# A fused decoder step on one NeuronCore: value pages of the second phase issued by GpSimd, and value quads moved ahead of the levels

## The chip, the cores and the metric

One NeuronCore of a Trainium2 chip runs the whole program. The metric is the device time of one launch in microseconds (us), the median of several runs. The profile is one more execution, taken by the hardware profiler. Engines are TensorE (PE, and PEld for its weight loads), VectorE (DVE), ScalarE (ACT), GpSimd (POOL) and SyncE (SP); SP only issues transfers here. SPq and POOLq are the sequencers of SP and POOL.

## What is computed

One layer of a hybrid decoder for a prompt of 2048 + 16 tokens and for 8 sampled sequences of one token each, all in float32. The part that matters here is the sampled sequences' attention over 8192 cached positions, which lie in pages of 128 positions x 512 floats (256 KB), found through a page table:

```python
xn = rms_norm(h, norm_w)
rq, rf, ri, rg, aq, ak, av, ag = split(xn @ w_in)        # 8 projections of 512 columns
o_rec = hgrn2_scan(rq, k_in(rf), ri, log_f(rf), S0)      # gated linear recurrence, 4 heads
k_all = concat(cache_k[page_table], ak)                  # 64 pages of each sampled sequence
v_all = concat(cache_v[page_table], av)
p = softmax(q @ k_all.T / 8)                             # two maps of each head
o_att = (p[0] - lam * p[1]) @ v_all
y = concat(rms_norm(o_rec) * silu(rg), rms_norm(o_att) * silu(ag))
out = h + y @ w_out
```

## The kernel before, in words

The prompt is cut into 16 tiles of 128 tokens and goes through two phases. The first phase (tiles 0 to 15) does the prompt's causal attention; the second (again tiles 0 to 15, then a tail of 24 rows) does its recurrence, in eight "levels" of a chunk, and the output projection. The eight sampled sequences run as side work beside both: 32 steps of 16 pages, four steps a sequence, where step `it` is tile `it` of the first phase and tile `it - 16` of the second. In each step VectorE multiplies 16 key pages with the query and sums (eight "key slots" of two pages, `key_slot`, L1361 and L1366, one buffer `Kt` of two slots), and TensorE multiplies 16 value pages of the sequence before it with its softmax weights, in four "value quads" of four pages (`value_quad`, L512). Tiles whose number is a multiple of 4 are the "opening" ones, where the side work changes to another sequence.

The value buffer `Vt` holds exactly one quad: four pages, in two halves. The next quad's pages may be asked for only when the quad before has been multiplied (semaphore `v_used`), and the quad waits at its head until both halves have landed. TensorE issues in order, so a late page stops all that stands behind the quad.

Who issues the pages. In the first phase SP issues key pages (`slots` with `ORDER_K`, L2100), and POOL issues value pages (`value_pages`, L1958: four page numbers are read into registers, a wait on `v_used`, four transfers). In the second phase SP issues both, in an order written out by hand (`ORDER_B`), one queue: `K0 V0 V1 K1 K2 K3 K4 K5 V2 V3 K6 V4 V5 K7 V6 V7`, where each name is a pair of pages. Ahead of K6 stands `turned_x` (L2152), the load of the input tile after next, 512 KB, which waits until all four projections of the present tile are done. POOL's own work in the second phase is little: it stores the finished output rows (L2062, L2069, L2070, after a wait on VectorE's final normalization L1751), waits for that store, loads the residual rows of a later tile (`load_x`, L357 and L358) and loads the attention output (L2067, after TensorE's transposes L820).

TensorE's order in a tile of the second phase (`b_tile`), non-opening: projections 1 and 0 (L747, 32 matmuls each), a wait, projection 3, quad 0, eight transposes (L762), projection 2, then level 0 (L863, and transposes L820) and levels 1 to 7 (four small matmuls each, L868). Behind levels 1, 2, 3 and 5 stands a quarter of the output projection of the tile before (L831), and behind levels 1, 4 and 7 stand quads 2, 4 and 6. Then come transposes (L881), the outputs (L888, L889) and the state update (L894). In an opening tile quad 0 stands inside `opening_front`, behind projection 3. VectorE makes each level's operands (L1799, L1800), takes each level's result (L2217), and works off key slots in between; in a non-opening tile key slot 6 stands ahead of level 2's operands.

In the first phase the order on TensorE around a tile's heads is written in `filler`, `scores` (L451, L456), `turn` (L465) and `values` (L480); the next tile's projections (`project_a`, L411) and the value quads are its fillers. In tiles 8 to 15 a head's row is cut into two pieces (c = 0 and 1); VectorE's `join` makes the piece's weights (L1412, L1413 for c = 0, L1416 for c = 1) and `norm_a` (L1422 to L1432) normalizes the tile before, and releases the first `values` of the tile by the semaphore `normed`. POOL's order there, for each tile t: pages of quad 0, store of xT and K, then in tile 14 the load of next-phase weights W[1] and W[0] (`next_weights`, L1966, 2 MB each, which wait for the last use of the weights they replace), the attention store (L2000, after `normed`), pages of quad 2 and quad 4, the store of V, and again in tile 14 W[2], pages of quad 6, W[3].

## Time and profile before

| | |
|---|---|
| time before, median of 3 runs | 2221.23 us (2218.32 to 2232.84) |
| the profiled execution | 2214.55 us, its span 2212.7 us |
| TensorE, VectorE, ScalarE, GpSimd busy | 90%, 73%, 23%, 10% of the span |
| mean granted TensorE clock | 0.950 |
| moved by DMA | 356.52 MB, mean 161 GB/s |
| first phase, second phase and tail | 0 to about 1101 us, about 1101 to 2212.7 us |

The median is 6.7 us above the profiled execution. Times in the rows are from the start of the span. "Idle before" is the time for which the engine stood still just ahead of an instruction, and the arrow names what ended it.

### The profile page before, as it was taken

Reading aid. Unit: us, or ns where it says so; the run is one execution under the profiler, and the core shown is the slowest. Engines: PE = TensorE matmul, PEld = TensorE weight load, DVE = VectorE, ACT = ScalarE, POOL = GpSimd, SP = SyncE. Lnnn points to the kernel's source line nnn. Section 1 sums busy time; section 2 is a strip of 40 time slices with the busy share of each in tenths; the row PEclk is TensorE's granted clock in tenths of the full one; section 3 lists DMA queues with packets and bytes.
Section 4 is the critical chain, followed back from the end, with each engine's and each line's share of the span. In section 5 each row is a group of like instructions: output and inputs, shape, how many; then the busy total and the mean of one; then the engine's idle time right before and its main releaser. Section 6 shows DMA issues by size and latency. Waiting matters only on the chain.

```text
span 2212.7 us, 31467 instructions
## 1 busy us (share of the span) xinstructions
PE 1981.8 (90%) x9530; PEld 1203.9 (54%) x9530; DVE 1623.0 (73%) x3477; ACT 518.9 (23%) x1280; POOL 229.0 (10%) x443
## 2 busy tenths in 40 slices
PE   6899999987989899877779999999989999999987
PEld 3444445543544454434557666666657766667443
DVE  2588778776777787758667886888778886888653
ACT  1233333332433343333301111111111111111100
POOL 0000122111111111011120000000000000000020
PEclk9999999999999999988889999999999999999988
DMA  6254466634534334454355553555545553655663
GB/s 223 92 167 148 149 217 201 198 116 141 168 125 148 124 118 136 143 181 167 124 174 166 177 174 109 191 177 177 175 138 178 175 186 105 195 174 173 185 213 119
DMA packets 165757, 356.52 MB, mean 161 GB/s; under 512 B 21040, under 2 KB 25920, under 8 KB 165600
## 3 DMA queue, kind: packets, MB, share of 16 engines
q1 hardware_dynamic: 131536, 240.41, 34.1%
q0 software_dynamic: 34064, 114.19, 15.6%
q8 instruction: 77, 1.26, 0.2%
q14 instruction: 80, 0.66, 0.1%
HBM read 322.52 MB, written 32.00 MB: 160 GB/s over the span
## 4 chain that ended last, share of the span: by engine, by line
PE 35%; DVE 8%; DMA 5%; SPq 2%; issue 2%; ACT 0%; DVEq 0%; ACTq 0%
PE PS L747 18%; PE PS L831 5%; DMA Vt<-in_cache_v_dram 4%; PE PD L512 3%; DMA Kt<-in_cache_k_dram 2%; DVE Kt L1361 2%; DVE sc L1366 2%; SPq L2100 1%; PE PS L744 1%; PE PS L868 1%; PE PO L888 1%; PE PS L948 1%; PE PO L889 1%; PE PS L894 1%; PE PS L906 1%
## 5 line engine op out<-in xcount | busy, mean ns | idle before, releaser
L411 PE MATMUL PT<-W,xT 128*128 128x512 f32 x960 | 432.9, 599 | 1.2 <-ACT xT L1008 1.1
L1361 DVE TENSOR_TENSOR Kt<-Kt,qb 128x1024 f32<-128x1024 f32 x256 | 312.2, 1219 | 42.9 <-DMA Kt<-in_cache_k_dram 42.4
L1366 DVE TENSOR_REDUCE sc<-Kt 128x16 f32<-128x1024 f32 x256 | 312.2, 1220 | 8.0
L747 PE MATMUL PS<-W,normw 128*128 128x256 f32 x1024 | 308.6, 383 | 0.0
L411 PEld LDWEIGHTS PT<-W,xT 128*128 128x128 f32 x960 | 177.3, 192 | 192.7 <-issue 190.6
L831 PE MATMUL PS<-region 128*128 128x512 f32 x512 | 232.1, 596 | 3.6 <-ACT region L1236 3.5
L747 PEld LDWEIGHTS PS<-W,normw 128*128 128x128 f32 x1024 | 197.5, 193 | 27.7
L1045 ACT ACTIVATE Pr<-PS,negm 128x512 f32<-128x512 f32 (+7 forms) x192 | 165.6, 866 | 163.3 <-DVE negm L1380 146.3
L512 PE MATMUL PD<-Vt,pst 128*8 128x512 f32 x912 | 123.8, 615 | 55.4 <-DMA Vt<-in_cache_v_dram 55.3
L456 PE MATMUL PS<-region,Q 64*128 64x512 f32 (+3 forms) x640 | 161.7, 620 | 0.0
L747 PE MATMUL PS<-W,xbuf 128*128 128x256 f32 x512 | 158.3, 392 | 0.8 <-DVE oX L1662 0.8
L1382 DVE TENSOR_REDUCE negm<-PS 128x1 f32<-128x640 f32 (+3 forms) x64 | 65.4, 1021 | 123.5 <-PE PS L456 123.5
L480 PE MATMUL PO<-region,PTs 128*128 128x128 f32 x1088 | 145.8, 284 | 7.3 <-issue 6.4
L747 PE MATMUL PS<-W,xT 128*128 128x256 f32 x512 | 152.3, 379 | 0.0
L480 PEld LDWEIGHTS PO<-region,PTs 128*128 128x128 f32 x1088 | 135.5, 197 | 26.5 <-issue 14.2
L831 PEld LDWEIGHTS PS<-region 128*128 128x128 f32 x512 | 92.3, 190 | 97.8 <-issue 91.8
L1958 POOL DMA_DIRECT2D Vt<-in_cache_v_dram x192 | 103.9, 541 | 363.5 <-PE PD L512 292.7
L1062 ACT ACTIVATE PTs<-PT 128x512 f32<-128x512 f32 (+3 forms) x160 | 85.2, 533 | 237.0 <-PE PT L465 233.3
L465 PEld LDWEIGHTS PT<-ident,Pr 128*128 128x128 f32 x544 | 65.3, 150 | 138.7 <-issue 127.3
L465 PE MATMUL PT<-ident,Pr 128*128 128x128 f32 x544 | 98.7, 301 | 40.4 <-DVE Pr L1413 37.5
L1380 DVE TENSOR_REDUCE negm<-PS 128x1 f32<-128x1024 f32 (+7 forms) x128 | 103.6, 851 | 39.3 <-PE PS L456 38.5
L747 PEld LDWEIGHTS PS<-W,xbuf 128*128 128x128 f32 x512 | 97.8, 196 | 21.1 <-issue 6.8
(377 smaller groups left out, 2348.8 us busy)
## 6 DMA issues: line engine op xcount, KB each, us to landing
Kt<-in_cache_k_dram SPq DMA_DIRECT2D x512, 256.0 KB, 3.6
Vt<-in_cache_v_dram SPq DMA_DIRECT2D x264, 256.0 KB, 3.6
Vt<-in_cache_v_dram POOLq DMA_DIRECT2D x192, 256.0 KB, 4.3
W<-in_w_in_dram SPq DMA_DIRECT2D x4, 2048.0 KB, 18.9
xT_scratch<-xT POOLq DMA_DIRECT2D x16, 512.0 KB, 6.2
W<-in_w_in_dram POOLq DMA_DIRECT2D x4, 2048.0 KB, 9.0
region<-in_x_prompt_dram POOLq DMA_DIRECT2D x16, 448.0 KB, 4.5
out_dram<-region POOLq DMA_DIRECT2D x16, 448.0 KB, 4.0
```

Source lines behind the costliest of these rows:

```text
L411: mm = pe.matmul(Pj, xT[:, c, :], W[:, b, c, :], start=(c == 0), stop=(c == DC - 1))
L456: mm = pe.matmul(PS[:, 2 * s + a, 0:n], Q[rows, h, :], KT[rows, h, first + o:first + o + n], start=not ends, stop=True, skip_group_check=ends)
L465: mm = pe.transpose(Pw[:, u:u + P], Pr[:, PLACE[t, h, c][0], o + u:o + u + P], ident[:, :])
L480: mm = pe.matmul(PO[:, h * P:(h + 1) * P], PTs[:, n % 2, u * P:(u + 1) * P], V[:, k + u, h * P:(h + 1) * P], start=(k + u == 0), stop=(k + ...
L512: mm = pe.matmul(PD[32 * j:32 * j + HC, :], pst[:, (2 * s + j) * HC:(2 * s + j + 1) * HC], ring[:, j // 2, j % 2, :], start=False, stop=Fa ...
L747: mm = pe.matmul(PS[:, BANK[b], a], rowsx, W[:, b, c, a], start=(c == 0 and a.start == 0), stop=(c == DC - 1), skip_group_check=True)
L831: mm = pe.matmul(PS[0:rows, b, :], yTs[:, c, 0:rows], Wo[:, c, b * G:(b + 1) * G], start=(c == 0), stop=(c == DC - 1))
L1045: act.activation(Pr[:, PLACE[t, h, c][s], 0:w], pair(s, w), ACT.Exp, bias=negm[:, h % 2, c, s:s + 1], accum_out=total).then_inc(p_done, 1)
L1361: link(ve.tensor_tensor(kp, kp, qb[:, :].unsqueeze(1).to_broadcast([P, 2, G]), ALU.mult))
L1366: ve.tensor_reduce(sc[:, g % 2, bass.ds(r16, 2), :].rearrange("p a c -> p (a c)"), kp.rearrange("p a (c d) -> p (a c) d", d=64), X, ALU.ad ...
L1380: ve.tensor_reduce(m, pair(s, w), X, ALU.max, negate=True).then_inc(m_done, 1)
L1958: pool.dma_start(Vt[:, u // 2, u % 2, :], vc[bass.ds(page, 1), :, :].rearrange("a t n -> t (a n)")).then_inc(va_load[u // 2], 16)
```

## The change

POOL issues the value pages of the second phase too: `value_pages` is no longer cut off at t = 16, and its calls stand in POOL's second-phase program between the stores and loads that are there already. SP is left with the key pages, and `turned_x` stays ahead of K6. The unused orders and the semaphores `v_load` go. The quads of a second-phase tile move: quad 0 of a non-opening tile stands behind projection 1, quad 2 behind projection 3 (in an opening tile behind projection 2), quad 4 behind level 1 (opening: 2), quad 6 behind level 5. In the first phase's tile 14 POOL takes the pages of quad 2 ahead of W[0] and the pages of quad 6 ahead of W[2], and W[3] goes to tile 15, behind the pages of quad 0. On VectorE, `norm_a` of the tiles 8 to 15 stands behind the join of the second piece, where it stood ahead of it.

```diff
@@ value_quad (TensorE)
                     for half in range(2):
-                        if g < 4:
-                            pe.wait_ge(va_load[half], (it * 4 + (s // 2 + 1 - 16)) * 32)
-                        else:
-                            pe.wait_ge(v_load[half], (it * 4 + (s // 2 + 1 - 64)) * 32)
+                        pe.wait_ge(va_load[half], (it * 4 + (s // 2 + 1 - 16)) * 32)
@@ b_tile (TensorE)
                 else:
-                    project(n, (1, 0))
+                    project(n, (1,))
+                    value_quad(it, 0, g)
+                    project(n, (0,))
                     pe.wait_ge(s_upd, after(t + 0, ONE_ON))
                     project(n, (3,))
-                    value_quad(it, 0, g)
+                    value_quad(it, 2, g)
                 qk_transposes(n)
                 project(n, (2,))
+                if t % 4 == 0:
+                    value_quad(it, 2, g)
...
-                    if l in (1, 4, 7):
-                        value_quad(it, {1: 2, 4: 4, 7: 6}[l], g)
+                    if l == (2 if t % 4 == 0 else 1):
+                        value_quad(it, 4, g)
+                    elif l == 5:
+                        value_quad(it, 6, g)
@@ first phase (VectorE)
                         join(t, h, 0)
+                        join(t, h, 1)
                         if h == 0:
                             norm_a(t - 1)
-                        join(t, h, 1)
@@ value_pages (GpSimd)
-                if t < 4 or t >= NT:
+                if t < 4:
                     return
@@ first phase (GpSimd)
                 value_pages(t, 0)
+                if t == NT - 1:
+                    next_weights(3)
...
                 if t == NT - 2:
                     next_weights(1)
-                    next_weights(0)
...
                 value_pages(t, 2)
+                if t == NT - 2:
+                    next_weights(0)
                 if t % 4:
                     value_pages(t, 4)
...
-                if t == NT - 2:
-                    next_weights(2)
                 if t % 4 == 0:
                     value_pages(t, 4)
                 value_pages(t, 6)
                 if t == NT - 2:
-                    next_weights(3)
+                    next_weights(2)
...
+            value_pages(NT, 0)
             pool.wait_ge(pv_done, NB + 5)
@@ second phase (GpSimd), behind the masks
+            value_pages(NT, 2)
+            value_pages(NT, 4)
+            value_pages(NT, 6)
+            value_pages(NT + 1, 0)
+            value_pages(NT + 1, 2)
+            value_pages(NT + 1, 4)
             pool.wait_ge(y_tr, 2)
             pool.dma_start(ycat[:, G:D], y_att_dram[1]).then_inc(ya_load, 16)
+            value_pages(NT + 1, 6)
+            value_pages(NT + 2, 0)
...
             for t in range(1, NT - 1):
+                value_pages(NT + t + 1, 2)
+                if (t + 1) % 4:
+                    value_pages(NT + t + 1, 4)
                 pool.wait_ge(y_tr, 2 * t + 2)
                 pool.dma_start(ycat[:, G:D], y_att_dram[t + 1]).then_inc(ya_load, 16)
+                if (t + 1) % 4 == 0:
+                    value_pages(NT + t + 1, 4)
+                value_pages(NT + t + 1, 6)
+                if t + 2 < NT:
+                    value_pages(NT + t + 2, 0)
                 pool.wait_ge(y_out, t + 1)
@@ second phase (SyncE)
-                slots(t + NT, ORDER_B, lambda: turned_x(t + 2) if t + 2 <= NT else None, 10)
+                slots(t + NT, lambda: turned_x(t + 2) if t + 2 <= NT else None, 6)
```

## Rows read from the trace of the kernel before

**Rows 1.** Waits, whole span: us in total, times, longest.
```profile
PE PD L512 <- DMA Vt<-in_cache_v_dram: 55.3, 26, 14.9
```

**Rows 2.** Line 512 alone: idle before it, 0 to 1100 us.
```profile
  DMA Vt<-in_cache_v_dram: 25.3, 4
```

**Rows 3.** Line 512 alone: idle before it, 1100 to 2080 us.
```profile
  DMA Vt<-in_cache_v_dram: 29.9, 22
```

**Rows 4.** Timeline of TensorE in tile 14: start, duration, instruction, [idle before].
```profile
926.50 2.02 PE L480 MATMUL PO<-region,PTs 128*128 128x128 f32 x16
...
934.53 0.29 PE L451 MATMUL PS<-causal,identb 128*128 128x128 bf16 x2 [2.14 <-ACT Pr L1045]
...
940.02 3.60 PE L411 MATMUL PT<-W,xT 128*128 128x512 f32 x8
958.48 1.90 PE L512 MATMUL PD<-Vt,pst 128*8 128x512 f32 x8 [14.86 <-DMA Vt<-in_cache_v_dram]
...
977.57 1.04 PE L512 MATMUL PD<-Vt,pst 128*8 128x512 f32 x8
```

**Rows 5.** Timeline of POOL in tile 14.
```profile
943.92 0.90 POOL L1966 DMA_DIRECT2D W<-in_w_in_dram  x1 [28.21 <-PE PT L411]
...
947.59 2.31 POOL L1958 DMA_DIRECT2D Vt<-in_cache_v_dram  x4 [2.22 <-issue]
```

**Rows 6.** Timeline of DVE in tile 14.
```profile
926.31 1.15 DVE L1416 SCALAR_TENSOR_TENSOR Pr<-Pr,wt 128x896 f32<-128x896 f32 x1
...
948.13 1.22 DVE L1366 TENSOR_REDUCE sc<-Kt 128x16 f32<-128x1024 f32 x1
964.10 2.35 DVE L1380 TENSOR_REDUCE negm<-PS 128x1 f32<-128x1024 f32 x2 [14.74 <-PE PS L456]
```

**Rows 7.** Engines by stretch: busy us (count) of PE, PEld, DVE, ACT, POOL, clock, DMA, GB/s.
```profile
944.00:960.00 16.00, 1.52 (x8) 0.15 (x8) 5.29 (x5) 0.25 (x1) 3.54 (x6) 0.55 0.77 280
```

**Rows 8.** Chain that ended last, second phase: first three projections of two tiles.
```profile
1229.76 20.72 PE PS L747 x96
...
1287.60 20.72 PE PS L747 x96
```

**Rows 9.** Timeline of a non-opening tile, 1225 to 1290 us.
```profile
1236.92 0.55 POOL L2062 DMA_DIRECT2D out_dram<-region  x1 [32.20 <-DVE region L1751]
...
1241.48 0.54 POOL L358 DMA_DIRECT2D region<-in_x_prompt_dram  x1
...
1259.42 0.33 SPq L2152 DMA_DIRECT2D xbuf<-xT_scratch  x1
...
1261.95 0.68 PE L868 MATMUL PS<-Pr 128*128 128x128 f32 x4 [0.79 <-DVE Pr L1800]
...
1264.56 1.22 DVE L1361 TENSOR_TENSOR Kt<-Kt,qb 128x1024 f32<-128x1024 f32 x1 [1.14 <-DMA Kt<-in_cache_k_dram]
...
1267.85 0.68 PE L868 MATMUL PS<-region 128*128 128x128 f32 x4 [0.81 <-DVE region L1800]
...
1282.50 0.43 DVE L2217 COPY_PREDICATED Pr<-Pr,PS 128x256 f32<-128x256 uint32 x1
...
1283.29 1.04 PE L512 MATMUL PD<-Vt,pst 128*8 128x512 f32 x8 [1.05 <-DMA Vt<-in_cache_v_dram]
```

**Rows 10.** Timeline of TensorE, opening tile of 1345 to 1418 us: two quads.
```profile
1397.24 1.04 PE L512 MATMUL PD<-Vt,pst 128*8 128x512 f32 x8 [2.53 <-DMA Vt<-in_cache_v_dram]
...
1413.74 1.04 PE L512 MATMUL PD<-Vt,pst 128*8 128x512 f32 x8 [0.60 <-DMA Vt<-in_cache_v_dram]
```

**Rows 11.** Waits of TensorE, first tile of the second phase, 1110 to 1172 us.
```profile
PE PD L512 <- DMA Vt<-in_cache_v_dram: 7.8, 3, 5.1
```

**Rows 12.** Waits of POOL, whole span: reading page numbers ahead of value pages.
```profile
POOL Vt L1958 <- issue: 64.3, 29, 3.8
```

**Rows 13.** DMA issues: engine, count, KB each, median us to landing.
```profile
Vt<-in_cache_v_dram SPq DMA_DIRECT2D x264, 256.0 KB, 3.6
Vt<-in_cache_v_dram POOLq DMA_DIRECT2D x192, 256.0 KB, 4.3
```

More of the change, by code:

```diff
@@ L30 @@
 READ = 4
-ORDER_A = "K0 V0 V1 K1 K2 V2 V3 K3 K4 V4 V5 K5 K6 V6 V7 K7".split()
-ORDER_OPEN = "K0 V0 V1 K1 K2 K3 K4 V2 V3 K5 K6 V4 V5 K7 V6 V7".split()
-ORDER_B = "K0 V0 V1 K1 K2 K3 K4 K5 V2 V3 K6 V4 V5 K7 V6 V7".split()
-ORDER_K = [f"K{s}" for s in range(SLOTS)]
 RSQRT_SEED = 1597463007.0
@@ L330, in build @@
         dve = sem("dve")
-        k_load = [sem("k_load0"), sem("k_load1")]; v_load = [sem("v_load0"), sem("v_load1")]
+        k_load = [sem("k_load0"), sem("k_load1")]
         va_load = [sem("va_load0"), sem("va_load1")]
@@ L2095, in page_numbers, with slots @@
                 return numbers
-            def page_pair(cache, dst, pair, s, free, uses):
-                need(sp, free, uses)
-                for u, page in enumerate(pair):
-                    sp.dma_start(dst[:, u, :], cache[bass.ds(page, 1), :, :].rearrange("a t n -> t (a n)")).then_inc(s, 16)
-            def slots(it, order, between=None, place=2):
-                for i, slot in enumerate(order):
-                    if i == place and between is not None:
-                        between()
-                    s = int(slot[1])
-                    u = 2 * (s % READ)
-                    if slot[0] == "K":
-                        if s % READ == 0:
-                            keys = page_numbers(16 * it + 2 * s, 2 * READ)
-                        page_pair(kc, Kt[:, s % 2], keys[u:u + 2], k_load[s % 2], k_used, after(8 * it + (s - 1), TWO_FREE))
-                    else:
-                        if s % READ == 0:
-                            values = page_numbers(16 * (it - 4) + 2 * s, 2 * READ)
-                        page_pair(vc, Vt[:, s % 2], values[u:u + 2], v_load[s % 2], v_used, after(4 * (it - 4) + s // 2, ONE_ON))
+            def slots(it, between=None, place=2):
+                for s in range(SLOTS):
+                    if s == place and between is not None:
+                        between()
+                    if s % READ == 0:
+                        keys = page_numbers(16 * it + 2 * s, 2 * READ)
+                    need(sp, k_used, after(8 * it + (s - 1), TWO_FREE))
+                    for u in range(2):
+                        sp.dma_start(Kt[:, s % 2, u, :], kc[bass.ds(keys[2 * (s % READ) + u], 1), :, :]
+                                     .rearrange("a t n -> t (a n)")).then_inc(k_load[s % 2], 16)
             load_tail(sp, xbuf, ax_in)
@@ L2135, in _ @@
             with sp.Fori(0, 4) as it:
-                slots(it, ORDER_K, lambda: next_x(it))
+                slots(it, lambda: next_x(it))
             with sp.Fori(4, NT - 2) as it:
-                slots(it, ORDER_K, lambda: next_x(it))
-            slots(NT - 2, ORDER_K)
+                slots(it, lambda: next_x(it))
+            slots(NT - 2)
             def turned_x(t):
@@ L2154, in turned_x @@
                     sp.dma_start(xbuf[:, 0:DC * TR], xT_dram[NT, :, 0:DC * TR]).then_inc(x_in[0], 16)
-            slots(NT - 1, ORDER_K, lambda: turned_x(0))
+            slots(NT - 1, lambda: turned_x(0))
             turned_x(1)
             for t in range(NT):
-                slots(t + NT, ORDER_B, lambda: turned_x(t + 2) if t + 2 <= NT else None, 10)
+                slots(t + NT, lambda: turned_x(t + 2) if t + 2 <= NT else None, 6)
             sp.wait_ge(v_used, after(4 * 28, ONE_ON))
```

## The prediction

> **What bounds the kernel now.** I read the page first, then the waits of TensorE, then line 512 alone in each phase, and then timelines of single tiles. TensorE is busy for most of the span (the table ahead), so its idle time is the thing to look for. The longest of its waits is line 512, the value quads, on their own pages: 55.3 us in 26 waits [rows 1]. The reader is to see two different shapes in it. In the first phase it is 25.3 us in only 4 waits [rows 2], and one of them, in tile 14, is 14.86 us [rows 4]. In the second phase it is 29.9 us in 22 waits [rows 3], small ones, about one in each tile. The change touches both, so I work them out apart.
>
> **Tile 14 of the first phase.** POOL stood for 28.21 us ahead of W[0], until 943.92, when TensorE had used the old W[0] (project_a, L411, ended at 940.02 + 3.60 = 943.62) [rows 4, 5]. The pages of quad 2 stand behind it in POOL's queue and were issued from 947.59 on, while TensorE had reached the quad at 943.6 and started it at 958.48 [rows 4, 5]. They also shared the transfer engines with the 2 MB of W[0]: 280 GB/s and a DMA share of 0.77 in that stretch [rows 7]. After the change POOL's queue has, ahead of these pages, only the attention store, which waits for `normed`, that is for VectorE's `norm_a`, done when L1416 starts at 926.31 [rows 6]. The page numbers take 64.3 / 29 = 2.2 us [rows 12], four issues 2.3 us [rows 5], the last page 4.3 us from its issue at about 931 [rows 13]: landed at about 935, 8 us before TensorE comes. The wait of 14.86 us goes. What is late next is VectorE: it had finished its key slots at 949.35 and stood 14.74 us for the scores [rows 6], so both engines move up together and the gain is 14.7 us. The stall also ended at the lower clock level, 0.55 in that stretch [rows 7], and the quad behind it took 1.90 us where others take 1.04 [rows 4, 9]; VectorE caps that, so I count nothing more. Quad 4's pages now stand behind W[0]; they would land about when quad 2's did, near 958.5, and quad 4 stood 977.57 - 958.48 = 19.1 us behind quad 2 on TensorE [rows 4], so it comes at 943.6 + 19.1 = 962.7, 4 us later. W[2] and W[3] move behind pages that they stood ahead of; all is loaded long before 1101 us. Bounds of this part: 4 us (if quad 4 waited 10) to 16 us.
>
> **The swap on VectorE.** In tile 14 `norm_a` ends about when L1416 starts, 926.31, and TensorE starts `values` at 926.50 [rows 4, 6]. With L1416 (1.15 us here) ahead of it, `normed` comes 0.8 to 1.2 us later in each of eight tiles, since the second piece is 640 to 1024 columns wide. But TensorE stands 2.14 us for ScalarE a little later, at 934.53 [rows 4], and that wait is set by VectorE's total, which the swap doesn't change. So I cost it at 0.5 us in sum; bounds 0 and 8 x 1.1 = 9 us.
>
> **Non-opening tiles of the second phase (12).** One tile takes 1287.60 - 1229.76 = 57.84 us [rows 8]. TensorE's idle time in it is small: 0.79 ahead of level 1, 0.81 ahead of level 2, 1.05 ahead of quad 6 [rows 9]. Quads cost no more elsewhere, 1.02 us each, so only waits count. Quad 2 now stands ahead of projection 2, which ends 1.02 us later. That hides the wait ahead of level 1. But the wait ahead of level 2 is the chain end of projections at 1259.42, `turned_x`, K6 behind it in SP's queue, VectorE's slot at 1264.56, level 2 at 1267.85 [rows 9]: 8.4 us that the change leaves as they are. So level 2 comes at 1268.87, 1.02 us later, with one quad more done. From there on the quad behind level 4 is gone and one stands behind level 5, which cancel; quad 6 with its wait of 1.05 behind level 7 goes: L881 starts at 1267.85 + 1.02 + (1283.29 - 1.05 - 1267.85) = 1283.26, where it started about 1283.29 + 1.02 = 1284.3. Then the outputs wait for VectorE's last copy, which before ended at 1282.93 [rows 9] and now follows level 7, about 1 us later: 0.25 us lost. Gain 0.75 us.
>
> Against it stands quad 2's supply. POOL starts its store at 1236.92, and its load of residual rows ends at 1242.02; later tiles have one more store of 0.5 us. Then come page numbers 2.2, issues to 1247, the last one at 1246.5, landing 4.3 later at 1250.8 [rows 5, 9, 12, 13]. TensorE reaches quad 2 at 1229.76 + 20.72 + 1.02 = 1251.5 [rows 8]. A slack of 0.7 us is too little to be met in every tile, and key pages are now in flight beside it, so I take off 0.15: 0.6 us a tile, 12 x 0.6 = 7.2 us. Bounds for a tile: -1.0 (pages 2 us late) and +2.5 (K6 early enough not to bind, 0.75 + 1.75 us).
>
> The Trainium skill (DMA: Bandwidth & Descriptors, "Issuing engine by pattern") would give simple loads to SyncE and calls that path generally faster. The medians agree, 3.6 us for SP and 4.3 us for POOL [rows 13]. By that alone each page comes 0.7 us later, just the slack above.
>
> **Opening tiles (3) and the first tile.** In an opening tile two quads wait, 2.53 and 0.60 us [rows 10]. The levels there carry key slots and are VectorE's, so what the first wait leaves is mostly taken by VectorE; I count the last wait and a little, 0.8 us each, 2.4 in all (bounds 0 and 3 x 3.1 = 9). The first tile waited 7.8 us in three waits [rows 11]; its levels have no output quarters, so VectorE, which makes their operands, is close behind. Its pages can be issued as soon as POOL has made its masks, earlier than behind K5 in SP's queue. I take half, 4 us (bounds 0 and 7.8).
>
> **The sum.** 14.7 - 0.5 + 7.2 + 2.4 + 4.0 = 27.8 us. The profiled execution took 2214.55 us (span 2212.7 and 1.9 around it), so one like it comes to 2186.8. The median of the runs stood 6.7 us above the profiled execution; taken over, that is 2221.2 - 27.8 = 2193.4 us.
>
> **Rivals.** (a) The K6 chain falls apart: with value pages out of SP's queue K6 lands earlier, and level 2 no longer waits. For: the chain had 1.14 us of VectorE idle [rows 9]. Against: `turned_x` still stands ahead. The 12 tiles would gain 2.4 us instead of 0.6: 22 us more, 2172 us.
>
> (b) Tile 14 trades its wait: pages of quad 4 behind W[0] come late. For: the last pages of quad 2 took 10.9 us from 947.59 beside W[0] [rows 4, 5]. Against: 4 us of slack. Or the swap of VectorE is paid in full. Either costs about 8 us: 2201 us, a change within 1%.
>
> (c) Slower: POOL's queue is the new bound. Quad 2's pages stand behind POOL's store, its wait and its load in 11 tiles, and all of projection 2 and K6 stand behind quad 2. With the slack of 0.7 us and a gain of 0.75, a tile is slower once the pages take 1.5 us more than 4.3. At the rate seen beside W[0], some 9 us for the last page [rows 4, 5, 7], quad 2 waits 4 us, each of 11 tiles loses 3.3 us instead of gaining 0.6: 43 us less gain, 2236 us. Against: the second phase's traffic is lighter than in that stretch, and the same four pages on POOL's queue made only four long waits in the whole first phase [rows 2].
>
> (d) The change of queue gains nothing: transfers bound it, so pages land no sooner. Then only tile 14's reordering is left, 14 us: 2207 us. The Trainium skill says so (DMA: Bandwidth & Descriptors, "Issuing engines are not separate DMA queues"): all issuers share the same 16 transfer engines, and another issuer saves only issue time. What speaks against it here is that the waits are for order in a queue.
>
> **How the numbers follow.** Chances: forecast 0.55, (a) 0.12, (b) 0.13, (c) 0.06, (d) 0.14. The range 2170 to 2212 us holds the forecast's own spread (some 10 us either way), (a), (b) and (d), and leaves out (c) and the tails. 1% of the time before is 22 us, about what a measurement of this kernel can tell from no change, so faster means under 2199. The forecast is 6 us under that line, and some 0.50 of its 0.55 with it; (a) is well under it, and a little of (b): 0.65. (d), most of (b) and a part of (c), whose 2236 is still within 1%, make 0.31. The rest of (c), with pages another microsecond late, is 0.04.
>
> **What would show it.** Tile 14: no wait of over 3 us ahead of line 512, and VectorE's 14.74 us gone. Second phase: the quads' wait falls from 29.9 to under 8 us; non-opening tiles take about 57.2 us, with VectorE's wait ahead of K6 grown to about 2 us and TensorE's ahead of level 2 to about 1.7. It is wrong if quad 2 waits for pages by more than a microsecond in most tiles, if tiles take 55 us or 58, or if tile 14 waits at quad 4.

## The result, and the profile after

The changed kernel took 2233.13 us in the median of 20 runs (2218.56 to 2242.08), the kernel before 2224.72 us (20 runs on the same chip): ratio 1.0044, with a 95% interval of 1.0030 to 1.0057. I had forecast 2193.4 us; it became 8.4 us slower. The profiled execution took 2228.51 us, its span 2226.5.

The first cut is by stage. Columns are as in [rows 7]; each line but the first ends where the second phase starts (its first projection) or ends (the first projection of 24 rows). Before:

```profile
0.00:880.00 880.00, 784.91 (x3618) 409.19 (x3618) 635.16 (x1250) 303.55 (x744) 120.65 (x235) 0.96 0.48 155
880.00:1101.81 221.81, 168.51 (x990) 98.95 (x989) 149.16 (x267) 78.60 (x165) 29.89 (x52) 0.86 0.44 148
1101.81:2080.34 978.53, 913.87 (x4413) 647.45 (x4414) 778.79 (x1719) 124.21 (x331) 57.04 (x117) 0.97 0.53 168
```

After:

```profile
0.00:880.00 880.00, 783.07 (x3600) 408.54 (x3601) 631.31 (x1241) 300.37 (x737) 120.12 (x234) 0.96 0.48 155
880.00:1095.04 215.04, 172.52 (x1006) 99.84 (x1004) 153.09 (x276) 81.00 (x173) 32.22 (x57) 0.87 0.45 153
1095.04:2092.58 997.54, 923.89 (x4412) 644.96 (x4413) 781.13 (x1719) 124.22 (x331) 193.39 (x369) 0.97 0.51 165
```

In these two profiles the first phase became 6.8 us shorter and the second 19.0 us longer, 10.0 of them in TensorE's busy time with the same number of matmuls, the other 9.0 in its idle time. GpSimd is busy for 193 us where it was for 57: that is its 252 more transfers.

**Tile 14.** The edit did there what it was to do. TensorE, then GpSimd, in the timeline of after, tiles 14 and 15:

```profile
938.42 0.29 PE L447 MATMUL PS<-causal,identb 128*128 128x128 bf16 x2 [0.77 <-ACT Pr L1044]
...
945.82 1.04 PE L505 MATMUL PD<-Vt,pst 128*8 128x512 f32 x8
...
963.64 1.04 PE L505 MATMUL PD<-Vt,pst 128*8 128x512 f32 x8
...
1004.23 1.08 PE L461 MATMUL PT<-ident,Pr 128*128 128x128 f32 x4 [9.83 <-DVE Pr L1412]
```

```profile
934.81 2.33 POOL L1957 DMA_DIRECT2D Vt<-in_cache_v_dram  x4 [2.60 <-issue]
946.19 0.90 POOL L1965 DMA_DIRECT2D W<-in_w_in_dram  x1 [9.06 <-PE PT L407]
...
985.84 2.30 POOL L1957 DMA_DIRECT2D Vt<-in_cache_v_dram  x4 [14.84 <-PE PD L505]
988.13 0.90 POOL L1965 DMA_DIRECT2D W<-in_w_in_dram  x1
```

The pages go out at 934.81, 11 us before W[0], and quad 2 no longer waits. From the scores to quad 2 it took 958.48 - 934.53 = 23.95 us before [rows 4]; it takes 945.82 - 938.42 = 7.40 now, 16.55 less: the wait of 14.86, and 1.7 in the matmuls ahead of it, which had a granted clock of 0.81 before and have 1.00 now. Quad 4 at 963.64 doesn't wait either. But from quad 2 to the start of the second phase it now takes 1095.04 - 945.82 = 149.2 us where it took 1101.81 - 958.48 = 143.3. The last line of each fence shows where: in tile 15 the load of W[3], 2 MB, goes out at 988.13 right behind value pages, and TensorE then stands 9.83 us for VectorE (4.72 at this place before). VectorE itself stood 5.00 us for a key page:

```profile
1000.52 1.22 DVE L1360 TENSOR_TENSOR Kt<-Kt,qb 128x1024 f32<-128x1024 f32 x1 [5.00 <-DMA Kt<-in_cache_k_dram]
```

**The second phase.** The waits of TensorE and one of VectorE in it (us in total, times, longest). Before, beside [rows 3]:

```profile
PE PS L868 <- DVE region L1800: 14.4, 12, 3.1
...
PE PS L868 <- DVE Pr L1800: 5.4, 8, 2.1
...
DVE Kt L1361 <- DMA Kt<-in_cache_k_dram: 31.5, 26, 2.7
```

After:

```profile
PE PD L505 <- DMA Vt<-in_cache_v_dram: 19.5, 14, 3.4
PE PS L865 <- DVE Pr L1799: 16.6, 15, 3.1
PE PS L865 <- DVE region L1799: 15.0, 9, 4.3
...
PE PO L887 <- DVE Pr L2225: 5.0, 15, 0.4
PE PT L880 <- DVE Pr L1818: 4.9, 4, 1.4
...
DVE Kt L1360 <- DMA Kt<-in_cache_k_dram: 49.3, 32, 4.1
```

The quads' wait fell from 29.9 to 19.5, and three others took its place: the levels' wait for VectorE grew from 19.8 to 31.6, two new ones stand behind level 7, where quad 6 had stood (9.9 together), and VectorE's own wait for key pages grew by 18. Summed over the twelve plain (non-opening) tiles, TensorE's wait ahead of level 1 went from 0.8 to 11.9 us and that ahead of level 2 from 11.0 to 8.0; VectorE's wait at key slot 3 went from 10.6 to 26.9, and at slot 6, which stands ahead of level 2, from 19.9 to 12.1. One tile shows how they hang together. The timelines of GpSimd, VectorE and TensorE in after, from quad 0 at 1728.29 on:

```profile
1728.60 0.51 POOL L2086 DMA_DIRECT2D out_dram<-region  x1 [8.64 <-DVE region L1750]
...
1732.79 0.50 POOL L353 DMA_DIRECT2D region<-in_x_prompt_dram  x1 [3.13 <-DMA out_dram<-region]
...
1736.99 2.31 POOL L1957 DMA_DIRECT2D Vt<-in_cache_v_dram  x4 [3.17 <-issue]
```

```profile
1743.88 1.22 DVE L1360 TENSOR_TENSOR Kt<-Kt,qb 128x1024 f32<-128x1024 f32 x1 [4.05 <-DMA Kt<-in_cache_k_dram]
...
1754.40 1.23 DVE L1360 TENSOR_TENSOR Kt<-Kt,qb 128x1024 f32<-128x1024 f32 x1 [2.15 <-DMA Kt<-in_cache_k_dram]
```

```profile
1743.90 1.05 PE L505 MATMUL PD<-Vt,pst 128*8 128x512 f32 x8 [0.56 <-DMA Vt<-in_cache_v_dram]
...
1757.69 0.79 PE L865 MATMUL PS<-Pr 128*128 128x128 f32 x4 [3.05 <-DVE Pr L1799]
1758.27 5.23 PE L824 MATMUL PS<-region 128*128 128x512 f32 x8
```

Quad 2's pages were free to go when quad 0 ended, at about 1729.3. They went out almost 8 us later, behind the store, the wait for it, the load and a page-number read (3.17 us of "issue"). So they were in flight together with key pages; VectorE waited 4.05 us for these and 2.15 us for a later slot's, whose flight fell beside quad 4's pages. It reached level 1 late, TensorE stood 3.05 us for it, and the output quarter behind that wait took 5.23 us where others take 3.60. Of the eight plain tiles that follow a plain one, this was one of three long ones: from quad 0 to quad 0 five took 57.2 to 58.4 us and three 60.3 to 61.1, 58.9 in the mean, where the kernel before took 57.6.

In the opening tiles the wait for pages moved from quad 2 (2.5 to 2.9 us before) to quad 4 (2.7 to 3.4). GpSimd and TensorE in one of them, whose quad 2 starts at 1377.51:

```profile
1380.82 0.54 POOL L2079 DMA_DIRECT2D region<-y_att_scratch  x1 [14.46 <-PE PT L813]
1385.36 2.29 POOL L1957 DMA_DIRECT2D Vt<-in_cache_v_dram  x4 [4.00 <-issue]
```

```profile
1391.62 1.04 PE L505 MATMUL PD<-Vt,pst 128*8 128x512 f32 x8 [2.72 <-DMA Vt<-in_cache_v_dram]
...
1406.67 0.65 PE L880 MATMUL PT<-ident,Pr 128*128 128x128 f32 x4 [1.35 <-DVE Pr L1818]
```

Quad 4's pages go out 6.8 us behind the end of quad 2, because the attention load stands ahead of them in GpSimd's order and waits for TensorE, and their page numbers are read behind it. Counted from a tile's first projection to the next one's, the first tile took 67.2 us where it took 70.5, the three opening ones 74.9 in the mean where 72.5, and the twelve plain ones 58.8 where 57.5: -3.3 + 7.1 + 15.3 = 19.1 us, the stage's 19.0.

### The profile page after: what moved, and what is told of

The parts are those of the page before. It is cut to its first block, busy times and chain, and to the rows that moved or that the text cites. A ratio compares the mean times of both kernels' runs of the same rounds, so it can differ in the third digit from the quotient of the medians.

```text
span 2226.5 us, 31563 instructions
## 1 busy us (share of the span) xinstructions
PE 1995.5 (90%) x9530; PEld 1201.8 (54%) x9530; DVE 1625.4 (73%) x3477; ACT 518.2 (23%) x1280; POOL 367.2 (16%) x699
## 4 chain that ended last, share of the span: by engine, by line
PE 26%; DVE 12%; DMA 7%; issue 5%; POOLq 1%; SPq 1%; POOL 1%; ACT 0%; DVEq 0%; ACTq 0%
PE PS L824 8%; PE PS L740 6%; DMA Kt<-in_cache_k_dram 3%; DVE Kt L1360 2%; DVE sc L1365 2%; PE PD L505 2%; DMA Vt<-in_cache_v_dram 2%; PE PS L865 2%; PE PS L737 1%; DMA out_dram<-region 1%; POOLq L1953 1%; DVE region L1750 1%; PE PO L887 1%; DVE Pr L2225 1%; DVE region L1828 1%
## 5 line engine op out<-in xcount | busy, mean ns | idle before, releaser
L1957 POOL DMA_DIRECT2D Vt<-in_cache_v_dram x448 | 242.4, 541 | 852.7 <-PE PD L505 697.0
L824 PE MATMUL PS<-region 128*128 128x512 f32 x512 | 239.4, 611 | 2.3 <-ACT region L1235 2.3
L476 PE MATMUL PO<-region,PTs 128*128 128x128 f32 x1088 | 146.2, 285 | 12.1 <-issue 10.5
```

The lines of the kernel that those rows point to most:

```text
L476: mm = pe.matmul(PO[:, h * P:(h + 1) * P], PTs[:, n % 2, u * P:(u + 1) * P], V[:, k + u, h * P:(h + 1) * P], start=(k + u == 0), stop=(k + ...
L824: mm = pe.matmul(PS[0:rows, b, :], yTs[:, c, 0:rows], Wo[:, c, b * G:(b + 1) * G], start=(c == 0), stop=(c == DC - 1))
L1957: pool.dma_start(Vt[:, u // 2, u % 2, :], vc[bass.ds(page, 1), :, :].rearrange("a t n -> t (a n)")).then_inc(va_load[u // 2], 16)
```

## The experiments

My theory after this reading: value pages now fly beside key pages and make them late. Rivals: the quads' new places, GpSimd's queue itself, and for the first phase W[3] and the swap. Ratios are to the kernel before on the same chip, with 95% intervals; "second phase" is as above, in one profiled execution.

**1. The first-phase parts alone.** The kernel before with the change's first-phase edits and nothing else, in the core:

```diff
                         join(t, h, 0)
+                        join(t, h, 1)
                         if h == 0:
                             norm_a(t - 1)
-                        join(t, h, 1)
...
+                if t == NT - 1:
+                    next_weights(3)
...
-                    next_weights(0)
...
                 value_pages(t, 2)
+                if t == NT - 2:
+                    next_weights(0)
```

> The kernel before with the first-phase parts of the change alone (the join ahead of norm_a, the next weights' loads on GpSimd's queue in their new places); the second phase keeps SyncE's queue and the old places of the quads. Theory 1 (the second phase loses by the value pages' new queue): the first phase keeps its 6.8 us and the second stays at 978 us, so 6 to 8 us below before, ratio about 0.997. Rival (the longer second phase comes from where it starts, or from the weights arriving later): the second phase is again near 997 us, ratio about 1.004.

Measured: 0.9946 (0.9922 to 0.9969), 12 us less; second phase 980.5 us. So the loss is in the second phase's own edits, and the next three kernels take them apart.

**2. GpSimd's queue with the old places of the quads.**

```diff
-                    if l == (2 if t % 4 == 0 else 1):
-                        value_quad(it, 4, g)
-                    elif l == 5:
-                        value_quad(it, 6, g)
+                    if l in (1, 4, 7):
+                        value_quad(it, {1: 2, 4: 4, 7: 6}[l], g)
```

(quad 0 back behind projection 3 too, and GpSimd asks for quad 4's pages behind the attention load.)

> The changed kernel, GpSimd issuing all value pages, with the second phase's quads back in their old places (behind projection 3, and in levels 1, 4 and 7). Theory 1 (the queue: key pages now share the engines with value pages in flight and land late): the second phase stays near 997 us, VectorE's wait for key pages near 49 us, ratio about 1.004. Rival 2 (the places of the quads): the second phase returns to about 978 us and the key waits to about 31, ratio about 0.997. If each is half: about 988 us, ratio 1.000.

Measured: 1.0006 (0.9992 to 1.0021); second phase 994.0 us, VectorE's key waits 34.1. None of the three cases as put: the ratio is that of the half-and-half case, the second phase is not. The queue alone costs 0.0060 x 2221 = 13 us against the first experiment, though the key waits are hardly longer in sum; the new places cost the other 8 us, up to 1.0044, by the ratios. The profiles show less of that: 994.0 us here, 997.5 and 993.1 in two kernels with the changed second phase (after and experiment 8). What the queue did is seen at two places. The first is quad 6. Timeline of quad 4 and quad 6 on TensorE, and of the issue between them, with SyncE's queue (first experiment):

```profile
1571.58 1.04 PE L512 MATMUL PD<-Vt,pst 128*8 128x512 f32 x8
1578.47 1.04 PE L512 MATMUL PD<-Vt,pst 128*8 128x512 f32 x8 [0.87 <-DMA Vt<-in_cache_v_dram]
```

```profile
1572.82 1.88 SPq L2101 DMA_DIRECT2D Vt<-in_cache_v_dram  x4
```

and with GpSimd's:

```profile
1522.63 1.04 PE L505 MATMUL PD<-Vt,pst 128*8 128x512 f32 x8
1530.32 1.04 PE L505 MATMUL PD<-Vt,pst 128*8 128x512 f32 x8 [1.67 <-DMA Vt<-in_cache_v_dram]
```

```profile
1524.37 2.29 POOL L1951 DMA_DIRECT2D Vt<-in_cache_v_dram  x4 [7.08 <-PE PD L505]
```

GpSimd starts 1.74 us behind quad 4 where SyncE starts 1.24 behind it, and takes 2.29 us for four issues where SyncE takes 1.88: the last page goes out 0.9 us later, and quad 6 waits 0.8 longer. Over 16 tiles its wait is 1.8 us in the mean, where it was 0.9. A longer wait also has a second price. Two stretches from quad 6 to the next quad 0 in this kernel, behind waits of 1.53 and 1.86 us:

```profile
1220.40:1245.37 24.97, 24.96 (x132) 21.35 (x133) 19.33 (x44) 3.57 (x13) 3.73 (x7) 1.00 0.45 146
1278.79:1305.38 26.59, 26.59 (x133) 22.97 (x133) 18.35 (x42) 3.57 (x13) 4.21 (x8) 0.94 0.46 140
```

The second has a granted clock of 0.94 in its mean, so a part of it at the lower of the two levels, 1.2 GHz, and takes 1.6 us more for the same work. Five of eleven such stretches did that here, none of eleven in the first experiment.

The second place is the levels. The queue saved 15.9 us of waits for pages in the opening tiles and the first one, but the levels' waits for VectorE rose from 23.3 to 37.2 us. In the first tile 5.4 us of page waits went and 5.5 came back at the levels: there VectorE was next in line. In the plain tiles no such wait had gone, and yet the wait ahead of level 1 rose from 2.0 to 9.4 us in sum. There it is key slot 5, the last one ahead of level 1: from the issue of its first page to the landing of both it takes 6.4 us in the mean where it took 4.8, and VectorE's wait for it rose from 0.2 to 8.9 us. At slot 6 it waits 3.9 us less, which hides this in the sum of the key waits.

**3. The last quad's pages back on SyncE**, all else as in 2:

```diff
-                if t < 4:
+                if t < 4 or (t >= NT and first == 6):
                     return
...
+                if isinstance(it, int) and it >= NT:
+                    values = page_numbers(16 * (it - 4) + 12, 4)
+                    need(sp, v_used, after(4 * (it - 4) + 3, ONE_ON))
+                    for u in range(4):
+                        sp.dma_start(Vt[:, u // 2, u % 2, :], ...).then_inc(v_load[u // 2], 16)
```

> The kernel with GpSimd's queue and the old places of the quads, with the pages of the last quad of each second-phase tile (slots 6 and 7) given back to SyncE. Theory 1b (with the old places the loss is that GpSimd's pages reach that quad 0.8 us later than SyncE's did, 1.7 against 0.95 us of wait in each of 15 tiles, and that the clock then falls for part of the next stretch in six tiles): the waits of these quads return to about 0.95 us, the granted clock stays at 1.00 in the stretch behind them, and the second phase goes from 994 to about 978 us, ratio 0.994 to 0.996. Rival (two queues in flight at once slow each other, whichever engine issues): the second phase stays within 4 us of 994 and the ratio near 1.000.

Measured: 0.9940 (0.9918 to 0.9961), second phase 977.8. The waits of all quads fall from 28.9 to 13.2 us, and the stretch behind quad 6 keeps its clock:

```profile
1276.10:1301.10 25.00, 25.00 (x136) 21.38 (x140) 19.44 (x43) 3.57 (x13) 4.22 (x8) 1.00 0.54 169
```

So the issuer of quad 6's pages is worth 16 us here, and the rival as I put it, 994 whichever engine issues, is out. That two queues in flight cost nothing doesn't follow. Slot 5 is late here too, beside quad 2's pages, in the timelines of GpSimd, VectorE and TensorE:

```profile
1244.13 2.31 POOL L1956 DMA_DIRECT2D Vt<-in_cache_v_dram  x4 [10.53 <-PE PD L510]
```

```profile
1252.59 1.22 DVE L1359 TENSOR_TENSOR Kt<-Kt,qb 128x1024 f32<-128x1024 f32 x1 [2.60 <-DMA Kt<-in_cache_k_dram]
```

```profile
1255.88 0.68 PE L866 MATMUL PS<-Pr 128*128 128x128 f32 x4 [2.77 <-DVE Pr L1798]
```

Its pages take 6.6 us in the mean, and TensorE waits 12.9 us ahead of level 1 in the plain tiles, where the first experiment had 4.8 and 2.0. By tiles (first projection to first projection) the twelve plain ones take 58.6 us where the first experiment took 57.5, and the three opening ones 68.9 where it took 73.8: some 13 us lost and 15 gained, and the sum looks like one queue's.

**4. The new places with one queue on SyncE**, in two orders:

```diff
-ORDER_B = "K0 V0 V1 K1 K2 K3 K4 K5 V2 V3 K6 V4 V5 K7 V6 V7".split()
+ORDER_B = "K0 K1 V0 V1 K2 K3 V2 V3 K4 K5 K6 V4 V5 K7 V6 V7".split()
```

> The first-phase parts of the change and the new places of the quads in the second phase, but SyncE issues all pages of the second phase in one queue, in the order K0 K1 V0 V1 K2 K3 V2 V3 K4 K5 K6 V4 V5 K7 V6 V7. Theory 1 (the queue): the second phase is 978 us or shorter, ratio 0.994 to 0.997, key waits at most 35 us. Rival 2 (the places): near 997 us, ratio about 1.004, with waits of TensorE for VectorE behind levels 4 and 7 where no quad stands any more. Rival 3 (one queue can't serve these places, the head of the queue waits): above 1000 us, with waits of both kinds of pages above those of before.

Measured: 1.1121 (1.1100 to 1.1142), TensorE waiting 233.8 us for value pages.

> The new places with one queue on SyncE once more, in another order: K0 K1 V0 V1 K2 V2 V3 K3 K4 K5 V4 V5 K6 K7 V6 V7, so that no value page stands behind a key page that can only be issued once VectorE is inside the levels. If the 234 us of waiting in the first order were the place of V4 V5 and V2 V3 in the queue: they fall below 60 us and the ratio below 1.02. If one queue can't serve these places at all, since key pages and value pages come free at times that depend on each other: waits above 150 us again, ratio above 1.06.

Measured: 1.0642 (1.0596 to 1.0687), 130.7 us for value pages and VectorE 115.0 for key pages: the ratio of my second case, the waits between the two. By the orders, which I did not follow page by page, value pages that belong ahead of level 1 stood behind key pages that came free only inside the levels, or the other way round. These two orders don't serve the new places; others were not tried, so the pair doesn't say what the places cost with a queue that fits.

**5. Half the bytes.** In the changed kernel, and in that of experiment 2, the second phase's value pages are loaded to half their columns:

```diff
+                    cols = 256 if t >= NT else 512
-                    pool.dma_start(Vt[:, u // 2, u % 2, :], vc[bass.ds(page, 1), :, :]
+                    pool.dma_start(Vt[:, u // 2, u % 2, 0:cols], vc[bass.ds(page, 1), :, 0:cols]
```

> The changed kernel, where each value page of the second phase is loaded only to half its columns (the other half of the tile keeps older values), so that GpSimd issues as many transfers of half the bytes; key pages are whole. Theory 1 (transfers in flight together: value pages take the key pages' share of the engines): VectorE's wait for key pages falls from 49 us to 35 or less, TensorE's waits behind level 1 with it, TensorE's for value pages from 19.5 to under 12, and the second phase from 997 to 980 to 988 us. Rival 2 (the places alone): key waits fall little, the waits behind levels 4 and 7 (10 us) and the slower output projection stay, second phase above 990 us. Rival 3 (GpSimd's queue itself, its turns and its page-number reads): key waits stay above 45 us and value waits above 16.

> GpSimd's queue and the old places of the quads, with each value page of the second phase loaded only to half its columns (the other half of the tile keeps older values). Beside the changed kernel with half pages (second phase 972 us, ratio 0.9925) it tells what the new places are worth when pages are hardly late. If the places are worth the 9.6 us that the prediction gave them (0.6 and 0.8 us per tile) less nothing: second phase about 981 us, ratio 0.996 to 0.998. If what the new places save in waits for pages they lose behind levels 4 and 7, where no quad stands between the levels: second phase within 3 us of 972, ratio 0.991 to 0.994.

Measured: 0.9925 (0.9905 to 0.9946) in the new places and 0.9836 (0.9808 to 0.9863) in the old; second phase 972.0 and 958.0 us. The stretch and TensorE's waits in it, new places:

```profile
1094.77:2066.76 971.99, 915.80 (x4412) 642.19 (x4412) 780.71 (x1719) 124.28 (x331) 193.39 (x369) 0.98 0.42 136
```

```profile
PE PT L880 <- DVE Pr L1818: 4.9, 4, 1.4
PE PO L887 <- DVE Pr L2226: 4.6, 14, 0.4
PE PD L505 <- DMA Vt<-in_cache_v_dram: 4.4, 4, 1.3
```

and old places:

```profile
1098.28:2056.28 958.00, 910.50 (x4412) 645.55 (x4412) 780.47 (x1719) 123.82 (x331) 192.65 (x369) 0.98 0.44 137
```

```profile
PE PD L505 <- DMA Vt<-in_cache_v_dram: 0.9, 2, 0.7
...
PE PO L881 <- DVE Pr L2217: 0.7, 2, 0.4
```

Two things follow. Bytes in flight are worth 25.5 us of the changed kernel's second phase, more than I expected, and 36.0 in the old places (994.0 to 958.0). In the new places they went mostly out of the quads' own wait (19.5 to 4.4) and TensorE's busy time (923.9 to 915.8); the key waits only fell from 49.3 to 42.1, not to 35. TensorE's waits ahead of level 1 in the plain tiles did go, 11.9 to 1.8 us, but ahead of level 2 it waited 13.4 for 8.0. So my theory of late key pages holds for a part. And both expectations on the places failed: with pages hardly late, the new ones are 14.0 us slower than the old. The first of them was wrongly put: the 9.6 us were mostly waits for pages, and half pages take these out of the old places too. 8.7 us of the 14.0 are idle time, where the waits behind level 7 alone (L880 and L887) are 9.5 us against 1.1 in the old places; 5.3 are busy time, 4.1 of them in the outputs behind those waits (54.0 us against 49.9 for the same 256 matmuls).

**6. Quad 2's pages ahead of the load.** The changed kernel with

```diff
+            value_pages(NT + 2, 2)
...
                 pool.dma_start(yp[t * P:t * P + 112, :], hbuf[16:P, :]).then_inc(yb_st, 16)
+                if t + 2 < NT:
+                    value_pages(NT + t + 2, 2)
                 pool.wait_ge(yb_st, t * 32 + 16)
                 load_x(pool, hbuf, hx_load, t + 1)
...
             for t in range(1, NT - 1):
-                value_pages(NT + t + 1, 2)
```

> The changed kernel, where GpSimd issues the pages of each second-phase tile's second quad (slots 2 and 3) right behind the output's store, ahead of its wait for that store and of the load of the next tile's input, instead of behind both. Theory 3 (in the changed kernel these pages are free to go when the first quad is done, but go out 8 to 10 us after that quad's start, behind the store, 3 us of waiting for it, the load and a page-number read; that makes them late and puts them on top of key pages 3 to 5): they go out 2 to 5 us after the quad's start, TensorE's wait for value pages falls from 19.5 to under 12 us, VectorE's for key pages from 49 to under 42, the second phase from 997 to 980 to 988 us, ratio 0.995 to 1.000. Rival 1 (pages of both kinds in flight are late whenever they go out): the waits move to other key pages, the second phase stays within 4 us of 997, ratio 1.003 to 1.005.

Measured: 0.9982 (0.9968 to 0.9997), 14 us less than the changed kernel by the ratios, 6.4 in the second phase of the profiles (991.1). The quads' wait fell to 8.9 us as expected, so GpSimd's order held these pages back. The other half failed: key waits rose to 55.7 us. Here is one, with what was in flight, in the timelines of GpSimd, SyncE and VectorE:

```profile
1477.24 2.34 POOL L1957 DMA_DIRECT2D Vt<-in_cache_v_dram  x4 [5.12 <-issue]
1479.57 0.51 POOL L353 DMA_DIRECT2D region<-in_x_prompt_dram  x1
```

```profile
1479.56 1.16 SPq L2125 DMA_DIRECT2D Kt<-in_cache_k_dram  x2
```

```profile
1487.48 1.23 DVE L1360 TENSOR_TENSOR Kt<-Kt,qb 128x1024 f32<-128x1024 f32 x1 [5.18 <-DMA Kt<-in_cache_k_dram]
```

Two key pages were issued behind 1 MB of value pages and beside 0.5 MB of input, and VectorE got them 7.9 us after the first was issued; the median for a key page in the changed kernel is 3.4 us. This is the effect of my theory, seen directly.

**7. That load put off** until quad 4's pages have gone out:

```diff
-                load_x(pool, hbuf, hx_load, t + 1)
...
                     value_pages(NT + t + 1, 4)
+                    next_input(t)
```

> The kernel with the second quad's pages ahead of the input's load, and with that load (512 KB) put off until the third quad's pages have gone out. Theory 1 (transfers in flight together: the load and the second quad's pages, 1.5 MB within 4 us, hold up the key pages, whose longest wait rose to 5.2 us there): VectorE's wait for key pages falls from 55.7 to under 46 us, its longest from 5.2 to under 4, TensorE's waits behind level 1 from 32.6 to under 27, the second phase from 991 to 982 to 987 us, ratio 0.994 to 0.997. Rival (the four value pages alone are enough to hold up the keys): key waits stay above 52 us and the ratio within 0.9975 to 0.999.

Measured: 1.0015 (0.9991 to 1.0039), second phase 994.3. The key waits did what the theory said, 44.3 us, the longest 3.5. The time did not: the levels still waited 29.4 us, and the quads' wait rose to 11.6, two in opening tiles to 3.9 and 4.4. So fewer microseconds of key waits are not by themselves worth time here. In the plain tiles TensorE's wait ahead of level 1 fell from 11.9 to 4.8 us, 4.1 came back ahead of level 2, and a tile took 58.1 us for 58.3; the opening tiles took 76.1 for 74.1 and ate it. That is one profile each, and why the opening tiles grew isn't settled.

**8. The swap, and W[3].** The changed kernel with `norm_a` back between the joins:

> The changed kernel with norm_a back between the two joins of the first head. Theory 5 (the swap costs the 3.9 us by which tiles 11 to 13 of the first phase run later than before): 4 us below the changed kernel, ratio to before about 1.0025, and tile 14's first quad at about 917.6 us. Rival (that shift is chance, or comes from the transfers): no difference, ratio about 1.0044, first quad of tile 14 at about 921.5 us.

Measured: 1.0032 (1.0013 to 1.0051); tile 14's first quad at 922.2 us. The interval takes in both ratios, 1.0025 and 1.0044, so the swap has no price that can be told. Nor is it the cause of the later tiles. The kernel of experiment 1 with W[3] later:

```diff
-                if t == NT - 1:
-                    next_weights(3)
...
                 value_pages(t, 6)
+                if t == NT - 1:
+                    next_weights(3)
```

> The kernel with the first-phase parts alone, but the last of the four weight loads (2 MB) stands behind tile 15's last value pages instead of behind its first. Theory 4 (that load, in flight with tile 15's key and value pages, makes VectorE wait 4.3 us for a key page and TensorE 9.2 us for VectorE at 1004 us): both waits fall to 1 us and to about 5, the first phase ends 4 to 5 us sooner (1088 to 1089 us), and the ratio goes from 0.9946 to about 0.992 to 0.993. Rival (the transposed tile that SyncE loads there, or the value pages themselves): the wait stays at 4 us and the ratio at 0.9946.

Measured: 0.9948 (0.9928 to 0.9967), not to be told from 0.9946. The trace does show it: TensorE's wait in tile 15 is back from 9.2 us to

```profile
1000.82 1.09 PE L465 MATMUL PT<-ident,Pr 128*128 128x128 f32 x4 [4.86 <-DVE Pr L1413]
```

and from quad 2 of tile 14 to the second phase it takes 143.4 us, as before (143.3), where experiment 1 took 146.3. So W[3] in its changed place costs about 3 us (5.9 in the profile of after alone), below what a measurement of 0.2% either way can tell.

**9. What helped, together**: experiments 3 and 8's last edit.

> The two edits that helped or did no harm, together: the old places of the quads, GpSimd's queue for the second phase's value pages but the last quad's pages on SyncE, and the last weight load behind tile 15's pages. If the two add: second phase near 978 us, the stretch from tile 15's first quad to the first projection of the second phase near 96 us where it was 98.6 with the load in its changed place, ratio 0.991 to 0.994. Rival (the weight load's place gives nothing that a measurement can tell, and the mixed queue alone is what counts): ratio 0.994 as before, within its interval.

Measured: 2194.25 us against 2222.90, ratio 0.9869 (0.9848 to 0.9889), faster than both kernels. Second phase 974.7 us; from quad 2 of tile 14 on 143.3. That is more than the 3 us of W[3] on top of 0.9940; the profiles explain 3 + 3 us, the rest not, and there were only 4 runs of this kernel.

## Why the prediction was wrong

**Tile 14: right.** Forecast 14.7 us with a bound of 16; 16.55 measured there, the wait of 14.86 and 1.7 us of matmuls ahead of it that ran at a higher clock, which I had not counted; and nothing late at quad 4. What I left out is the next sentence of that step, "W[2] and W[3] move behind pages that they stood ahead of; all is loaded long before 1101 us". I asked when the load is needed and not what it collides with: about 3 us came back in tile 15, 5.9 in the profile of after. With the swap, forecast at 0.5, these parts were to give 14.2 us; alone they gave 12 (7 to 17).

**The second phase: wrong by sign.** Forecast 13.6 us less (7.2 + 2.4 + 4.0), measured 22 more by the ratios (1.0044 - 0.9946 = 0.0098 of 2223) and 19.0 in the profiles. Three steps failed:

- "Key pages are now in flight beside it, so I take off 0.15." That term was the mis-sized one, and the largest: the plain tiles, forecast to gain 7.2 us, lost 15.3, from 57.5 to 58.8 us each; with half the bytes in the same places they take 57.6. Key pages came late beside the value pages, and TensorE waited 11.9 us ahead of level 1, where I had the wait as hidden and where 1.8 are left with half the bytes; the matmuls behind such a wait were slower. My bound for a tile, 1.0 lost, was near the mean, 1.3. The slack of 0.7 us for quad 2's pages wasn't there either: the quad waited in ten of twelve tiles, 0.5 us in the median. A term that sits on so little slack should have been taken at its bound.
- "Quads cost no more elsewhere, 1.02 us each, so only waits count." A quad among the levels is also the cover under which VectorE makes the next operands. I saw this for quad 6 and put it at 0.25 us a tile, at line 888. In the plain tiles the runs show 0.33 there (L887); in the opening tiles they show 1.7, 1.35 of it at L880, which I had not counted. My gain of 0.75 was quad 6's wait of 1.05 less that loss, rounded. With pages hardly late that wait is gone from both places, so 0.25 should be lost; 0.8 was (57.6 us for a plain tile against 56.8), some 0.4 of it in slower matmuls.
- "I count the last wait and a little, 0.8 us each" for the opening tiles. They lost 2.4 each: the wait for pages moved to quad 4, whose pages stand behind the attention load in GpSimd's order, and the waits behind level 7 came on top. The first tile, at 4.0 us ("I take half"), came out nearer: 3.3 less than before, 1.5 less than in experiment 1, whose first tile took 68.7. VectorE was next in line there, as I had written.

**The rivals.** (c), at 0.06, was closest in time, 2236 us, and half right in mechanism: quad 2's pages do stand behind POOL's store, its wait and its load, which costs 14 us by the ratios of experiment 6 (6.4 in its profile) and not 43. I had bounded it from the rate beside W[0] and then held the second phase's lighter traffic against it. (d) is what is left when the second phase's edits are taken out: forecast 2207, measured 2207.24. (a) showed in part and gained nothing: with SP's queue to themselves, the key pages of slot 6 made VectorE wait less and level 2 with it, and the wait stood ahead of level 1 instead. I missed the place where the slower issuer acts at once: in [rows 13] I read the landing, 3.6 and 4.3 us, but not that GpSimd also starts later and takes longer per issue, 0.9 us for four pages.

The Trainium skill (DMA: Bandwidth & Descriptors, "Issuing engines are not separate DMA queues") says that transfers begun by different engines share the same 16 transfer engines and interleave, so that more issuers save issue time alone. The runs agree: two key pages 7.9 us behind their issue beside 1.5 MB of others, and half the bytes worth 25.5 us of the second phase. I had it as rival (d) at no gain. What I draw from it, and the page does not say: the hand-written queue let key slot 5's pages go ahead of quad 2's (4.8 us to landing), and two queues don't (6.4).

**How firm.** Shown by pairs of kernels: that the first-phase parts gain, that the queue and the places each lose, that quad 6's issuer and GpSimd's order ahead of quad 2 matter. Argued from single profiles: every split by tiles, levels and key slots, and how a late key page turns into a slow tile; experiment 7 says that it is not the whole of it. Second phases of the same code differ by some 4 us from profile to profile (978.5, 980.5 and 982.3 in before and the two kernels of experiments 1 and 8 that keep it; 997.5 and 993.1 with the changed one), so the places' price with whole pages is shown by the ratios alone.

## What to carry to other kernels

A wait that goes is worth only what the next engine in line leaves of it: before moving work off a stretch that two engines share, ask what it covered there. Transfers taken out of one hand-written queue lose their order against the others, so a load that must not be late should not share its time with one that may. An issuer's own lead, here 0.9 us for four pages, counts fully where a buffer holds just one set.

## What the runs showed of the hardware that I had not expected

- A wait of about 2 us could cost nearly as much again: at 1.53 us the stretch behind kept a granted clock of 1.00 (24.97 us), at 1.86 it had 0.94 (26.59 us). It is no sharp rule: of the eleven, one kept it behind 1.84 and another lost it behind 1.82.
- With value pages on a second queue the median key page landed sooner, in 3.0 us after its issue where it took 3.5 (experiments 2 and 1), and yet VectorE waited longer: the two pages of the one slot that flew beside quad 2's took 6.4 us for 4.8.
- Profiled executions differ by some 12 us before an edit that sets them apart acts: tile 14's first quad stood at 919.6 and at 931.6 us in experiments 6 and 7, whose first phases are the same code, at 917.6 in the kernel before and at 921.5 after. I read the 3.9 us as a cost until experiment 8; the first phases of two profiles can't be compared closer than that, stretches within them can (146.2 to 146.8 us from quad 2 of tile 14 in six kernels with the same code there, but 149.2 in that of after).
